# Modulation sums of twenty blocks moved to the query stages, and the norms' root by square root and reciprocal

## The reference

```python
def rms_norm(x, g):
    xf = x.astype(jnp.float32)
    y = xf * lax.rsqrt(jnp.mean(xf * xf, axis=-1, keepdims=True) + EPS)
...
    m = jax.nn.silu(cvec) @ w + b          # six modulation vectors of a layer, for context and latent
    return jnp.split(m[:, None, :], 6, axis=-1)
...
    hp = modulate(rms_norm(xp, norm_ffn_g[l]), mp[3], mp[4])
    xp = xp + mp[5] * peer(hp, peer_wq[l], peer_keys[l], peer_u[l], peer_v[l])
```

## Time and profile before

| what | value |
|---|---|
| median of the timed runs | 2504.21 us (3 runs, 2499.9 to 2505.34) |
| the profiled execution's own time | 2514.36 us |
| its span, first to last instruction | 2512.6 us |
| granted TensorE clock, mean | 0.963 |
| busy: PE, DVE, ACT, POOL | 2295.6, 1727.8, 912.1, 1162.9 us |
| moved by DMA | 771.15 MB |

### The profile page before, as it was taken

One profiled execution on the slowest core, in us unless ns is written; L12 is line 12 of the kernel. 1 busy time (PEld: TensorE's weight loads), 2 busy tenths in 40 slices (PEclk: granted clock), 3 DMA queues, 4 the chain that ended last, 5 costly groups with the idle time before them and its releaser, 6 DMA issues.

```text
span 2512.6 us, 38357 instructions
## 1 busy us (share of the span) xinstructions
PE 2295.6 (91%) x11829; PEld 1699.1 (68%) x11829; DVE 1727.8 (69%) x3913; ACT 912.1 (36%) x1695; POOL 1162.9 (46%) x673
## 2 busy tenths in 40 slices
PE   6797999999877999999989889999999999999998
PEld 3686999999874343343458479999999944444443
DVE  7986798888555666676748747998885344455555
ACT  3344446666542111111044444666665510000002
POOL 2623587777773222222229444777777821111110
PEclk9898999999998999999999899999999999999999
DMA  8423378999999999999933023679999999999994
GB/s 304 160 96 123 114 223 313 381 386 376 399 418 408 404 399 408 400 409 409 387 125 109 0 84 118 200 269 377 386 378 380 407 398 393 383 374 395 398 397 188
DMA packets 195778, 771.15 MB, mean 307 GB/s; under 512 B 21728, under 2 KB 22880, under 8 KB 160224
## 3 DMA queue, kind: packets, MB, share of 16 engines
q1 hardware_dynamic: 120512, 402.81, 43.0%
q0 software_dynamic: 36864, 268.45, 27.1%
q10 hardware_dynamic: 38304, 98.71, 10.1%
HBM read 701.08 MB, written 68.81 MB: 306 GB/s over the span
## 4 chain that ended last, share of the span: by engine, by line
PE 53%; DMA 20%; DVE 15%; POOL 5%; issue 5%; ACT 2%; SPq 0%; ACTq 0%; DVEq 0%; POOLq 0%
PE ps L1790 24%; DMA raw<-in_v 12%; PE ps L1553 7%; PE ps L1554 7%; PE ps L1555 7%; PE ps L1772 4%; DMA raw<-in_u 4%; POOL w_lo L603 4%; DVE ga L1088 2%; DVE ps L1289 2%; DVE ps L1370 1%; DVE work L1372 1%; PE ps L1725 1%; DMA uv_stat<-in_uv,picked 1%; ACT w_hi L729 1%
## 5 line engine op out<-in xcount | busy, mean ns | idle before, releaser
L603 POOL TENSOR_TENSOR w_lo<-raw,w_hi 128x1024 fp32r<-128x1024 f32 x330 | 796.8, 2421 | 512.8 <-ACT w_hi L729 511.5
L1790 PE MATMUL ps<-raw,work 128*128 128x512 f32 x2048 | 909.7, 605 | 63.7 <-DMA raw<-in_v 47.2
L1553 PE MATMUL ps<-h_hi,w_hi 128*128 128x256 f32 (+1 forms) x2560 | 776.9, 303 | 49.3 <-POOL w_lo L603 48.6
L1790 PEld LDWEIGHTS ps<-raw,work 128*128 128x128 f32 x2048 | 392.7, 194 | 579.4 <-issue 535.3
L1554 PE MATMUL ps<-h_lo,w_hi 128*128 128x256 f32 (+1 forms) x2560 | 756.5, 295 | 0.0
L1555 PE MATMUL ps<-h_hi,w_lo 128*128 128x256 f32 (+1 forms) x2560 | 756.1, 295 | 0.0
L1553 PEld LDWEIGHTS ps<-h_hi,w_hi 128*128 128x128 f32 x2560 | 494.3, 193 | 63.4 <-POOL w_lo L603 60.3
L1554 PEld LDWEIGHTS ps<-h_lo,w_hi 128*128 128x128 f32 x2560 | 495.0, 193 | 0.0
L1555 PEld LDWEIGHTS ps<-h_hi,w_lo 128*128 128x128 f32 x2560 | 493.9, 193 | 0.0
L729 ACT ACTIVATE w_hi<-raw 128x1024 fp32r<-128x1024 f32 x330 | 347.7, 1056 | 137.1 <-DMA raw<-in_u 64.7
L977 ACT ACTIVATE wgt<-dots (+1 forms) x256 | 53.1, 207 | 712.0 <-DVE uv_stat L1431 213.3
(11 more groups left out here) (201 smaller groups left out, 2521.7 us busy)
## 6 DMA issues: line engine op xcount, KB each, us to landing
raw<-in_u SPq DMA_DIRECT2D x256, 512.0 KB, 6.7
raw<-in_v SPq DMA_DIRECT2D x256, 512.0 KB, 8.7
a_dram<-ga ACTq DMA_DIRECT2D x128, 256.0 KB
g_dram<-work ACTq DMA_DIRECT2D x16, 2048.0 KB, 12.1
work<-a_dram ACTq DMA_DIRECT2D x120, 256.0 KB, 8.5
work<-in_mod_w SPq DMA_DIRECT2D x56, 512.0 KB, 10.3
hots<-in_mod_w SPq DMA_DIRECT2D x32, 512.0 KB, 3.6
raw<-in_wq SPq DMA_DIRECT2D x32, 512.0 KB, 3.5
```

What stands on the lines that cost most here:

```text
L603: nc.gpsimd.tensor_tensor(w_lo[:, m % RING, :], raw[:, m % RING, :], w_hi[:, m % RING, :].bitcast(F32), ALU.subtract).then_inc(lo_ready, 1)
L1553: mm(out, w_hi[:, s, cols], h_hi[:, k, first:], start=n == 0, stop=False)
L1790: last = mm(ps[:, Y_DENSE[NT - ND_TILES + t] + half, :], wf[:, b, t * P:(t + 1) * P], raw[:, s, half * 512:(half + 1) * 512], start=first, ...
```

## The change

Blocks 32 to 43 (12) are summed in layer 0's query stage and blocks 80 to 87 (8) in layer 1's, and no longer in the sweep, which keeps the 36 from 44 to 79: turn 0 loads as before, turns 1 and 2 half as many, the last turn 4 instead of 8. As the keys lie over `c` by then, SP stores `c` to DRAM after the last early modulation load, and loads it into `uv_work` (in layer 0 once the first out block is evacuated, in layer 1 once the sweep's gathered rows are used). VectorE sums 6 blocks ahead of the first list and 2 behind each list while there are any. The blocks go through the ring in `hots`; their loads stand between those of the wq blocks on SP. The root becomes one square root on ScalarE and a reciprocal on VectorE ahead of the Newton step; the table of the exponential is then loaded after the first norm.

```diff
+QUERY_MODS = (range(MOD_EARLY, MOD_EARLY + 12), range(SUM_BLOCKS - KC, SUM_BLOCKS))
+QUERY_FIRST, QUERY_EACH = 6, 2
+QUERY_AT = (4, 5, 6, 7, 8, 9, 12, 13)
+SWEEP_MODS = range(QUERY_MODS[0].stop, QUERY_MODS[1].start)
+MOD_ROUNDS = len(SWEEP_MODS) // MSLOTS
+OTHER_TURN = {0: 1, 2: 2}
...
+        c_rows = uv_work.rearrange("p (g d) -> p g d", g=2)
+        unread_q = wf[:, :, :].rearrange("p a t -> p (a t)").bitcast(BF16).rearrange("p (g d) -> p g d", g=2)
...
+            sp.wait_ge(c_ready, 3)
+            sp.dma_start(c_dram[:, :], c_all.rearrange("p g d -> p (g d)")).then_inc(c_stored, 16)
+            sp.wait_ge(proj_taken, R0["out"] + 1)
+            sp.wait_ge(c_stored, 16)
+            sp.dma_start(uv_work, c_dram[:, :]).then_inc(c_rows_loaded, 16)
             for layer in range(DEPTH):
+                blocks = QUERY_MODS[layer]
+                if layer:
+                    sp.wait_ge(rows_used, SLOTS)
+                    sp.dma_start(uv_work, c_dram[:, :]).then_inc(c_rows_loaded, 16)
                 stream(f"wq{layer}", 0, RING, RING)
...
-                stream(f"wq{layer}", RING, HS - RING, 4)
+                else:
+                    sp.wait_ge(conv_done, KC - CONV_DVE)
+                for n in blocks[:MSLOTS]:
+                    mod_load(n)
+                for m in range(RING, HS):
+                    stream(f"wq{layer}", m, 1, 1)
+                    if m in QUERY_AT[:len(blocks) - MSLOTS]:
+                        mod_load(blocks[MSLOTS + QUERY_AT.index(m)])
...
-                    turn(0, False, range(1, 4))
+                    turn(0, False, {1: 0, 2: 1, 3: 2})
                     with sp.Fori(1, TURNS - 1) as i:
-                        turn(i, False, range(4))
-                    turn(TURNS - 1, True, range(MOD_ROUNDS - 4 * (TURNS - 1)))
+                        turn(i, False, OTHER_TURN)
+                    turn(TURNS - 1, True, {0: OTHER_TURN[0]})
...
-                preload(ACT.Ln)
+                preload(ACT.Sqrt)
                 act.wait_ge(var_ready, roots[0])
-                settle(nc.scalar.activation(stat[:, 1, 0:width], stat[:, 0, 0:width], ACT.Ln))
-                nc.scalar.activation(stat[:, 2, 0:width], stat[:, 1, 0:width], ACT.Exp, scale=-0.5).then_inc(std_ready, 1)
+                nc.scalar.activation(stat[:, 1, 0:width], stat[:, 0, 0:width], ACT.Sqrt).then_inc(std_ready, 1)
...
+                if n == 0:
+                    preload(ACT.Exp)
...
                 v, r, t = (stat[:, s, 0:width] for s in (0, 2, 3))
                 dve.wait_ge(std_ready, n + 1)
+                settle(nc.vector.reciprocal(r, stat[:, 1, 0:width]))
                 settle(stt(t, r, -0.5, r, ALU.mult, ALU.mult))
...
+                def query_sums(first, count):
+                    for n in blocks[first:first + count]:
+                        for g in range(2):
+                            mod_group(0, 0, n // MSLOTS * MSLOTS, n % MSLOTS, g, rows=c_rows, out=unread_q)
+                        if n % MSLOTS == MSLOTS - 1:
+                            mod_bias(0, 0, n // MSLOTS * MSLOTS)
+
+                dve.wait_ge(c_rows_loaded, 16 * (layer + 1))
+                query_sums(0, QUERY_FIRST)
                 for q in range(HS // 4):
...
                     settle(last)
+                    query_sums(QUERY_FIRST + q * QUERY_EACH, QUERY_EACH)
+                dve.wait_ge(mod_ready, blocks.stop // MSLOTS)
```

More of the change, by code:

```diff
@@ L354, in build @@
         mod_summed = sem("mod_summed")
+        c_stored = sem("c_stored")
+        c_rows_loaded = sem("c_rows_loaded")
         mod_ready = sem("mod_ready")
@@ L425, in build @@
         out_stored = sem("out_stored")
+        c_dram = nc.dram_tensor("c_dram", (P, 2 * D), F32)
         a_dram = nc.dram_tensor("a_dram", (N_KEYS // 2, P, 2 * ND), F32).ap()
@@ L487, in mod_load_late @@
             def mod_load_late(k):
-                sp.dma_start(mod_late[:, k, :], one(io["mod_w"], MOD_EARLY + k)).then_inc(mod_raw[k], 16)
+                sp.dma_start(mod_late[:, k, :], one(io["mod_w"], SWEEP_MODS[k])).then_inc(mod_raw[k], 16)
             for dst, src in ((x[:, :, :], io["x"]), (mod_b[:, :], io["mod_b"]), (gains[:, :, :], io["gains"]),
@@ L545, in _ @@
                     sp.wait_ge(s_done, HS)
+                    sp.wait_ge(mod_summed, 2 * SWEEP_MODS.start)
                     conditioning()
@@ L563, in turn @@
                         if j // 8 in mods and j % 2:
[L564 to L567, removed]
+                            block, k = SWEEP_MODS.start + mods[j // 8] * MSLOTS, j % 8 // 2
+                            sp.wait_ge(mod_summed, i * (4 * MSLOTS) + 2 * (block + k + 1))
+                            sp.dma_start(mod_late[:, k, :], one(io["mod_w"], i * (2 * MSLOTS) + (block + MSLOTS + k))
                                          ).then_inc(mod_raw[k], 16)
                 if layer == 0:
-                    turn(0, False, range(1, 4))
+                    turn(0, False, {1: 0, 2: 1, 3: 2})
                     with sp.Fori(1, TURNS - 1) as i:
-                        turn(i, False, range(4))
-                    turn(TURNS - 1, True, range(MOD_ROUNDS - 4 * (TURNS - 1)))
+                        turn(i, False, OTHER_TURN)
+                    turn(TURNS - 1, True, {0: OTHER_TURN[0]})
                 else:
@@ L789, in gated @@
                 m0 = M0[name]
-                act.wait_ge(mod_ready, [MOD_EARLY - 2 * KC, SUM_BLOCKS][layer] // MSLOTS)
+                act.wait_ge(mod_ready, [MOD_EARLY - 2 * KC, SWEEP_MODS.stop][layer] // MSLOTS)
                 with act.Fori(0, 2) as i:
@@ L1077, in _, with mod_group @@
             dve.wait_ge(first_loaded, 5 * 16)
-            def mod_group(i, step, block, k, g, ring=mod_w, first=None):
+            def mod_group(i, step, block, k, g, ring=mod_w, first=None, rows=c_all, out=unread):
                 if k == 0 and g == 0:
@@ L1087, in mod_group @@
                 since(dve, mod_summed, i * (2 * step) + (2 * (block + k) + g - 1))
-                nc.vector.tensor_tensor_reduce(unread[:, g, :], ring[:, k, :],
-                                               c_all[:, g, :] if g or first is None else first, 1.0, 0.0,
+                nc.vector.tensor_tensor_reduce(out[:, g, :], ring[:, k, :],
+                                               rows[:, g, :] if g or first is None else first, 1.0, 0.0,
                                                ALU.mult, ALU.add, accum_out=sums[:, k, g:g + 1]).then_inc(mod_summed, 1)
@@ L1484, in turn @@
                                     dve.wait_ge(a_stored[s], 16 * (N_KEYS // 4))
-                            block = MOD_EARLY - MSLOTS + j // 8 * MSLOTS
-                            mod_group(i, TURN // 8 * MSLOTS, block, j % 8 // 2, j % 2, mod_late)
+                            block = SWEEP_MODS.start + mods[j // 8] * MSLOTS
+                            mod_group(i, 2 * MSLOTS, block, j % 8 // 2, j % 2, mod_late)
                             if j % 8 == 7:
-                                mod_bias(i, TURN // 8 * MSLOTS, block)
+                                mod_bias(i, 2 * MSLOTS, block)
                         if final and layer == 0 and j == SPAN + 8:
@@ L1493, in sweep @@
                 if layer == 0:
-                    turn(0, False, range(1, 4))
+                    turn(0, False, {1: 0, 2: 1, 3: 2})
                     with dve.Fori(1, TURNS - 1) as i:
-                        turn(i, False, range(4))
-                    turn(TURNS - 1, True, range(MOD_ROUNDS + 1 - 4 * (TURNS - 1)))
+                        turn(i, False, OTHER_TURN)
+                    turn(TURNS - 1, True, OTHER_TURN)
                 else:
@@ L1502, in sweep @@
                 if layer == 0:
-                    dve.wait_ge(mod_ready, SUM_BLOCKS // MSLOTS)
+                    dve.wait_ge(mod_ready, SWEEP_MODS.stop // MSLOTS)
                     at = (6 + 2) * KC
```

3 lines of the change are left out of this document (1 added, 2 removed).

## The result

The changed kernel takes 2545.67 us (median of 4 runs, 2539.87 to 2545.74) against 2504.78 for the kernel before. The medians are 40.9 us apart; the ratio estimated from the runs is 1.0152, 95% interval 1.0129 to 1.0175, which is 38 us (32 to 44) slower, where 26 were forecast. The median lies 0.7 us past the upper end of the forecast range, 2545; the difference lies inside it, since that end stands 40.8 us above the 2504.21 from which the forecast started. The profiled executions are only 25.5 us apart (spans 2512.6 and 2538.1): that of before was slower than all four of its timed runs, that of after the fastest of its four. Where the two measures differ, the timed runs say how much, the traces where.

The account below looks back on a forecast made before the run. The prediction took DMA, with TensorE close behind, to bound layer 0's sweep turns, and VectorE's chain the query stage without slack. Its terms, -13 + 28 + 5 + 4 + 1 + 1 = +26 us, gave 2530 us, range 2508 to 2545.

Parts of the forecast that it names:

- Sums and subtractions exclude each other: Layer 0's query stage: two-SBUF-operand sums and GpSimd subtractions take turns, 2.2 us per subtraction met; cost 28 us.
- the walk: Instruction-by-instruction count of VectorE in layer 0's query stage: lists starting near 255, 279, 300 and 328 us.
- the clock's 1: TensorE's granted clock of 0.50 lasting longer behind the longer wait for `gate_s`: 1 us.
- Layer 1: Layer 1's query stage: last list 8.6 us late, 3.8 us back at line 1404; cost 5, bounds 0 and 9.
- The sweep's gain: Layer 0's sweep: fewer modulation bytes save 11 us in turns 1 and 2 and 2 in turn 3, 13 in all.
- The root: Six roots: a 2.48 us reciprocal replaces some 1.8 us, 4 us slower in all; an extra table load 1 us.
- What was costed at nothing: Query stage: c's store and load delay wq loads and ScalarE, covered by VectorE's early sums; later loads under TensorE's wait.
- (a): Query stages: sums slip between subtractions and cost nothing; -8 us in all, 2496 us; chance 0.10.
- (b): Exclusion costs half (14 and 2) and the sweep follows bytes (-20): +2 in all, 2506 us; chance 0.08.
- (c): Roots: the reciprocal is as cheap as other instructions of its shape; +14 in all, 2518 us; chance 0.08.
- (d): Roots: the reciprocal costs 0.7 us more than the slope, each root 1.4; +30 in all, 2534 us; chance 0.12.
- (e): Sweep: turns are bound by the gathers' round trips, gain 5 us instead of 13; 2538 us; chance 0.10.

Follow-up runs that it names:

- the sums alone: The changed kernel with the old root (logarithm and exponential), so only the sums are moved: 1.0156 to the kernel before, 39 us over it.
- layer 0 alone: Old root; only the 12 blocks of layer 0's query stage moved, layer 1's 8 stay in the sweep: 1.0127 to the kernel before, 32 us over.
- the one with one operand: The changed kernel, its query-stage sums reducing the block itself without the product with c, same loads and waits: 1.0011 to the kernel before.
- c in SBUF and in PSUM: Sums moved, old root: c in SBUF 1.0156 to the kernel before; c copied to PSUM for the product 0.9990.
- the root-alone kernel: The kernel before with the new root and later load of the exponential's table, no sum moved: 1.0008 to the kernel before, 2 us.
- the other place: The changed kernel with turns 1 to 3's modulation blocks in each half turn's second eight v blocks: 1.0086 to the kernel before, 22 us over.

## Why the prediction was right, and where it wasn't

- **Sums and subtractions exclude each other** (+28 in layer 0, bounds 0 and 30): right in mechanism and nearly in size. The lists came about 2 us from the walk, but the starting point was 3.6 us late, and that was part of the 30.4; from it the sums made the last list 26.8 us late. TensorE's wait grew by 23.1 us in this trace, and by 28.0 with the sums alone and with layer 0 alone. The runs price both layers together: 35 us between the changed kernel and the one with one operand, 42 between the two kernels with the old root, c in SBUF and in PSUM; the forecast had 34 (28, layer 1's 5 and the clock's 1). The Trainium skill states the rule ("SBUF — State Buffer", section "Who interferes with whom"): a VectorE instruction with two SBUF inputs contends with a GpSimd instruction that reads SBUF; one with at most one, outside the modes that use two ports, doesn't. The traces agree: 2210 ns on average against 1210 and 1217.
- **Layer 1** (+5): the wait for `gate_s` grew by 3.6 us, and line 1404 gave its time back as forecast (4.35 us before, 0.56 now). Alone it cost 1.5 us in the timed runs, its part of the sweep's gain included.
- **The sweep's gain** (-13, bounds -5 and -23) is the step that failed. Turns 1 and 2 gave 4.8 us instead of 11 and the last turn nothing; by TensorE's own blocks it was 1.4 and 3.4, so some 5 of the 13 either way. I took the time of a turn from its bytes and from layer 1's turns of equal bytes, and didn't look where in the half turn the remaining loads stand: a turn has long and short rounds, and the bytes came out of the short ones. Moved by eight v blocks they gave 16 us in the same two turns (231.0 for 247.3). Differences of a few us between two traces are not firm: the sweep of the root-alone kernel has the code of before and was 3.8 us shorter (493.8 and 497.6).
- **The root** (+4, and 1 for the table): 2.48 us was taken for the reciprocal by the slope of two small ones; it took 2.55. Alone, the timed runs gave 2 us (-2 to 6). By the Trainium skill ("VectorE: DVE Perf Modes", sections "First, the fixed hardware budget" and "Specifications"), with a repeat count of 8 at 0.96 GHz, the estimate was 3.2 us; the 2.55 us measured are 6.4 such cycles an element, and the measurement decides.
- **What was costed at nothing**: SP stored c at 187.72 and loaded it at 194.40; the first wq block was converted at 200.56 and ScalarE was through at 203.8, times as forecast (200 and 204). But the cover that the forecast counted on, VectorE's early sums, wasn't whole: VectorE waited 2.50 us for ScalarE, met the first subtraction, and was 2.9 us late at the last out block. In the traces of the sums alone and of the other place, which have the same store and load, that block came at 206.32 and 206.22, as before. So the store and the load cost nothing in some executions and up to 3 us in one.
- **The rivals:** (a) falls by the stretched sums, (b) by 35 us for the exclusion, (c) and (d) by 2.55 us for the reciprocal. (e) was nearest: the sweep gave its 5 us, though not by the gathers' round trips, as the other place gave 16 with the same gathers.
- **Luck:** the forecast put its 26 us on the profiled execution, and the two profiled executions differ by 25.5. That is not the sum coming true: layer 1's sweep, whose code the change leaves alone, was 4.5 us shorter in the trace of after (469.1 us for 473.6), which fills in for half of the sweep's missing gain.
- **Open:** the profiled executions differ by 25.5 us and the timed ones by 38. The kernel with the sums alone shows the same (profiled 2535.68, median 2546.92). Which stage takes the rest in the timed runs no trace here shows.

## What to carry to other kernels

Before work is put into an engine's waits, see which ports the work needs and what the neighbour does in that stretch: here the plain durations fitted the waits to the tenth, and each GpSimd subtraction met added 2.2 us. An operand in PSUM in place of SBUF turned the same move from 39 us lost into none. Of loads that are left in a saturated stage, look which part of it takes longest before choosing which to take out: here the place of 20 loads was worth some 16 us, and 20 loads fewer an estimated 13.

## What the runs showed of the hardware that was not expected

A VectorE instruction of eight columns paid about the same price as a long one: the bias addition of 128x8 took 2.24 us beside a subtraction, and 0.17 without. A reciprocal of 384 columns costs 2.55 us, 4.6 times a multiplication of that shape (0.56), so that one activation and a table load less on ScalarE didn't pay for it (3.14 us for the root's part where VectorE waited 2.42).
